# Last expert round of a decoder trunk: scatter by matmul replaced by a DRAM scratch and indirect fetches per token

## What is computed

```python
logits = hf @ router_w + router_b
top_p, top_i = lax.top_k(softmax(logits), 2)          # 2 of 8 experts per token
gates = one_hot(top_i) * (top_p / sum(top_p))
for e in range(8):                                    # D_FF_EXPERT = 3584
    out = out + gates[:, e:e+1] * (silu(hf @ w_gate[e]) * (hf @ w_up[e])) @ w_down[e]
x = x + gate_mod * out                                # gated residual, gate_mod per channel
y = x * rsqrt(mean(x * x, axis=-1) + 1e-6) * final_norm_g
```

## Time and profile before

| | us |
|---|---|
| three runs | 1512.93, 1510.95, 1510.21 |
| median | 1510.95 |
| profiled execution: its span, first to last instruction | 1512.1 |
| TensorE busy, of the span | 1430.2 (95%) |
| last `e_down` (753) starts | 1491.42 |

### The profile page before, as it was taken

How to read it: one execution, slowest core, us unless ns; L and a number is a source line. 1 busy time by engine, 2 the same in 40 slices (tenths; PEclk the granted TensorE clock), 3 DMA queues, 4 the chain that set the end, 5 groups by cost and what they waited for, 6 DMA issues and landing times.

```text
span 1512.1 us, 44722 instructions
## 1 busy us (share of the span) xinstructions
PE 1430.2 (95%) x19890; PEld 1062.4 (70%) x19890; DVE 370.1 (24%) x1021; ACT 159.2 (11%) x378; POOL 137.5 (9%) x230
## 2 busy tenths in 40 slices
PE   4999999999998898999999989989989989999996
PEld 3887888888887787666567757767757755555554
DVE  2816230220203715111111111111111111113334
ACT  2103111101112203100000000000000000000001
POOL 0000043140300000000000000000000000000000
PEclk8999999999999999999999999999999999999999
DMA  9948595646328705759999999999999999999870
GB/s 385 422 165 333 194 372 216 262 188 247 140 84 356 313 0 232 326 193 426 426 421 410 426 426 395 426 426 408 427 425 407 424 427 405 413 426 394 361 308 29
DMA packets 44202, 493.91 MB, mean 327 GB/s; under 512 B 4896, under 2 KB 5152, under 8 KB 5792
## 3 DMA queue, kind: packets, MB, share of 16 engines
q1 hardware_dynamic: 41040, 475.02, 76.4%
q10 hardware_dynamic: 3024, 16.73, 2.7%
HBM read 478.10 MB, written 13.63 MB: 325 GB/s over the span
## 4 chain that ended last, share of the span: by engine, by line
PE 82%; DMA 12%; DVE 4%; ACT 1%; issue 1%; SPq 0%; POOL 0%; DVEq 0%; POOLq 0%
PE PS L744 30%; PE PS L443 20%; PE PS L753 15%; DMA ring<-in_expert_stream 9%; PE PS L598 5%; PE PS L427 2%; DMA arena<-in_expert_stream 2%; DMA ring<-in_dense_stream 2%; PE PS L762 2%; PE PS L724 1%; DVE arena L1052 1%; PE PS L652 1%; PE PS L568 1%; PE PS L580 1%; PE PS L475 1%; PE PS L417 1%
## 5 line engine op out<-in xcount | busy, mean ns | idle before, releaser
L744 PE MATMUL PS<-ring,arena 128*32 128x256 f32 x7040 | 405.4, 381 | 21.7 <-DMA ring<-in_expert_stream 13.1
L744 PEld LDWEIGHTS PS<-ring,arena 128*32 128x32 f32 x7040 | 251.5, 110 | 154.1 <-issue 16.9
L443 PE MATMUL PS<-arena,ring 128*128 128x256 f32 x1408 | 314.2, 384 | 4.3 <-ACT arena L855 2.7
L443 PEld LDWEIGHTS PS<-arena,ring 128*128 128x128 f32 x1408 | 269.9, 193 | 44.5 <-issue 6.3
L753 PE MATMUL PS<-ring,arena 128*32 128x256 f32 x4928 | 298.4, 381 | 0.8 <-DVE consts L1052 0.8
L753 PEld LDWEIGHTS PS<-ring,arena 128*32 128x32 f32 x4928 | 178.6, 111 | 91.4 <-issue 4.4
L744 PE MATMUL PS<-arena 128*32 128x256 f32 x2816 | 162.9, 382 | 10.7 <-DMA arena<-in_expert_stream 7.8
L1052 DVE TENSOR_TENSOR stat<-stat,PS 128x128 f32<-128x128 f32 x154 | 44.4, 288 | 505.3 <-ACT stat L1010 505.3
L1052 DVE TENSOR_TENSOR arena<-arena,PS 128x256 f32 (+1 forms) x123 | 55.3, 449 | 376.3 <-PE PS L443 236.5
L744 PEld LDWEIGHTS PS<-arena 128*32 128x32 f32 x2816 | 101.2, 111 | 63.9 <-DMA arena<-in_expert_stream 9.0
L1602 POOL COPY arena<-arena 128x256 f32 x153 | 61.3, 401 | 817.3 <-PE PS L744 768.8
(11 more groups left out here) (187 smaller groups left out, 603.4 us busy)
## 6 DMA issues: line engine op xcount, KB each, us to landing
ring<-in_expert_stream SPq DMA_DIRECT2D x136, 2048.0 KB, 19.9
ring<-in_dense_stream SPq DMA_DIRECT2D x105, 1024.0 KB, 7.8
arena<-in_expert_stream SPq DMA_DIRECT2D x32, 2048.0 KB, 23.2
ssm_scratch<-arena ACTq DMA_DIRECT2D x12, 1024.0 KB, 5.0
ring<-ssm_scratch SPq DMA_DIRECT2D x12, 1024.0 KB, 9.8
arena<-in_xt ACTq DMA_DIRECT2D x1, 1024.0 KB, 13.9
arena<-in_ssm_small ACTq DMA_DIRECT2D x1, 1024.0 KB, 9.1
out_t<-arena ACTq DMA_DIRECT2D x4, 256.0 KB, 2.6
```

Source lines behind the costliest of these rows:

```text
L443: mm = pe.matmul(PS[:, bank, j * T:(j + 1) * T], w[:, c, j * P:(j + 1) * P], moving[:, c, :], start=(c == 0), stop=(c == NC - 1))
L744: mm = pe.matmul(PS[32 * q:32 * q + 32, 0, 0:256], hbuf[:, c * BLK:(c + 1) * BLK], w[:, q * 256:(q + 1) * 256], start=(c == 0), stop=(c == ...
```

## The change

- **No scatter.** `spread_turn`, `reps`, `gtb`, `gate_rows` and `scatter` go. In the last round `keep` adds to `acc` as in the others, and `scale_block` (VectorE, one 128x256 product per block) multiplies by the per-channel gate `gf_quads`.
- **Gate row.** `gf_quads` is made at the start of round 1: VectorE writes the gate on 8 diagonals (in the first round, in place of `spread`), TensorE multiplies them by ones (8 matmuls, `gate_row`), VectorE copies four quarters out of PSUM.
- **Stores.** After the Silu of block j ScalarE waits for `y_scaled` of block j-1 and issues a DMA of that block (128 rows of 1 KB) to `y_scr`, 896 rows of 4 KB in DRAM, one row per slot. Before, in the dense stage, four DMAs fill `y_scr` with 3.67 MB of `xt_in`, so that every row holds something.
- **Fetch.** When all stores have landed GpSimd issues four indirect DMAs, each of 128 rows of 4 KB (one per token) to `ring`: two tiles of 128 tokens, two picks each. TensorE meanwhile transposes the residual to token rows (16 transposes, `turn_resid`).
- **Mix and norm, token by token.** VectorE: four products with add of 128x1024. ScalarE: Square with its sum along the row, then Sqrt of 128x1. VectorE: reciprocal of 128x1, two products of 128x512 per tile. Four output DMAs.

```diff
 # TensorE
-            def scatter(first=False, last=False):
-                for h in range(2):
-                    for q in range(4):
-                        rows = slice(BLK * q, BLK * q + BLK)
-                        mm = pe.matmul(PS[:, 4 + q, h * T:(h + 1) * T], accb[rows, h * P:(h + 1) * P], gtb[rows, :],
-                                       start=(first and h == 0), stop=last, skip_group_check=True)
+            def turn_resid():
+                for tt in range(2):
+                    for c in range(NC):
+                        mm = pe.transpose(PS[:, 4 + 2 * tt + c // 4, (c % 4) * P:(c % 4 + 1) * P], B[:, c, tt * P:(tt + 1) * P], ident)
+                mm.then_inc(x_turned, 1)
...
                         e_down(at)
-                        if rnd == ROUNDS - 1:
-                            pe.wait_ge(gt_ready, j)
-                            scatter()
...
 # ScalarE
+            for n in range(-(-MOST * BLK // T)):
+                rows = min(T, MOST * BLK - n * T)
+                act.dma_start(y_scr[n * T:n * T + rows, :], xt_in.rearrange("p (h d) -> (p h) d", d=D)[0:rows, :]).then_inc(y_filled, 16)
...
+            def store_block(j):
+                act.wait_ge(y_scaled, j + 1)
+                act.dma_start(y_scr[bass.ds(j * BLK, BLK), :].rearrange("i (q n) -> q i n", q=4),
+                              acc[:, bass.ds(j * 256, 256)]).then_inc(y_stored, 16)
...
+            with act.Fori(1, upto[-1]) as j:
+                act.wait_ge(gu_done, j + upto[-1] * (ROUNDS - 1) + 1)
+                silu().then_inc(silu_ready, 1)
+                store_block(j - 1)
+            store_block(upto[-1] - 1)
...
 # VectorE, last round
                     dve.wait_ge(down_done, j + blocks * rnd)
-                    if rnd < ROUNDS - 1:
-                        keep(wide_block(acc, j - 1), rnd).then_inc(acc_done, 1)
+                    keep(wide_block(acc, j - 1), rnd).then_inc(acc_done, 1)
                     dve.wait_ge(e_hid, j + blocks * rnd + 1)
                     turn_hid().then_inc(hidT_ready, 1)
                     if rnd == ROUNDS - 1:
-                        dve.wait_ge(e_scat, j + 1)
-                        keep_last(j - 1)
-                        dve.wait_ge(gt_ready, j)
-                        gate_rows(j - 1)
+                        scale_block(j - 1)
...
+            dve.wait_ge(x_turned, 1)
+            for t_ in range(2):
+                dve.wait_ge(y_back[t_], 16)
+                link(dve.scalar_tensor_tensor(y_mix[t_], y_rows[2 * t_], r2[6][:, t_:t_ + 1],
+                                              PS[:, 4 + 2 * t_:6 + 2 * t_, :].rearrange("p b n -> p (b n)"), ALU.mult, ALU.add))
+                dve.wait_ge(y_back[2 + t_], 16)
+                dve.scalar_tensor_tensor(y_mix[t_], y_rows[2 * t_ + 1], r2[7][:, t_:t_ + 1], y_mix[t_], ALU.mult,
+                                         ALU.add).then_inc(mixed_ready, 1)
...
 # GpSimd, behind its last block copy
+            pool.wait_ge(down_done, upto[-1] * ROUNDS)
+            pool.wait_ge(y_stored, upto[-1] * 16)
...
+            for t_ in range(2):
+                for k in range(2):
+                    pool.indirect_dma_start(out=y_rows[2 * t_ + k], out_offset=None, in_=y_scr[:, :],
+                                            in_offset=bass.IndirectOffsetOnAxis(ap=slots_i[:, 2 * k + t_:2 * k + t_ + 1], axis=0)
+                                            ).then_inc(y_back[2 * k + t_], 16)
```

More of the change, by code:

```diff
@@ L248, in trunk_kernel @@
         hg = arena[:, 0:MOST * 256]
-        h_tm, sel, places, spread = more[:, 0:2048], more[:, 2048:3840], more[:, 3840:4736], more[:, 4736:5760]
+        h_tm, sel, places = more[:, 0:2048], more[:, 2048:3840], more[:, 3840:4736]
         o = 0
@@ L265, in trunk_kernel @@
         over, nbs = take(48), [take(8) for _ in range(3)]
+        att_sum = take(4)
         slot_of = [take(2) for _ in range(2)]
@@ L727, in gather, with gate_row @@
                 mm.then_inc(e_gather, 1)
[L729 to L735, removed]
+            def gate_row():
+                pe.wait_ge(diag_ready, 1)
+                for c in range(NC):
+                    mm = pe.matmul(PS[:, 2 + c // 4, (c % 4) * P:(c % 4 + 1) * P], ones, g_diag[:, c * P:(c + 1) * P], start=True, stop=True)
+                mm.then_inc(gf_psum, 1)
             def gate_up(at, fresh):
@@ L773, in _ @@
             for rnd in range(ROUNDS):
-                if rnd == ROUNDS - 1:
-                    pe.wait_ge(part_zeroed, 1)
-                    pe.wait_ge(reps_ready, 1)
-                    scatter(first=True)
+                if rnd == 1:
+                    gate_row()
                 for e in range(EXPERTS):
@@ L812, in _ @@
             e_down(expert_at(ROUNDS - 1, EXPERTS - 1))
[L814 to L821, removed]
+            pe.wait_ge(hg_ready, GATHERS)
+            turn_resid()
         @block.scalar
@@ L1027, in _ @@
                     silu().then_inc(silu_ready, 1)
-            for rnd in range(1, ROUNDS):
+            for rnd in range(1, ROUNDS - 1):
                 with act.Fori(0, upto[-1]) as j:
@@ L1454, in _ @@
             link(tt(r2[7], r2[5], r2[6], ALU.mult))
[L1455 to L1458, removed]
+            for k in range(2):
+                s = dve.tensor_copy(slots_i[:, 2 * k:2 * k + 2], slot_of[k])
+            s.then_inc(slots_ready, 1)
+            dve.wait_ge(mod_taken, 5)
+            for c in range(NC):
+                s = dve.tensor_scalar(g_diag[:, c * P:(c + 1) * P], ident, part(3, 2)[:, c:c + 1], None, ALU.mult)
+            s.then_inc(diag_ready, 1)
             def col(a, at):
@@ L1475, in keep, with scale_block @@
                 return tt(dst, dst, PS[:, 1, 0:256], ALU.add)
[L1477 to L1486, removed]
+            def scale_block(j):
+                dve.wait_ge(acc_done, blocks * (ROUNDS - 1) + j + 2)
+                tt(wide_block(acc, j), wide_block(acc, j), gf_quads, ALU.mult).then_inc(y_scaled, 1)
             dve.wait_ge(items_ready, 1)
@@ L1501, in _ @@
                 turn_hid().then_inc(hidT_ready, 1)
[L1502 to L1505, removed]
+                if rnd == 1:
+                    dve.wait_ge(gf_psum, 1)
+                    for q in range(4):
+                        s = dve.tensor_copy(gf_quads[32 * q:32 * q + 32], PS[32 * q:32 * q + 32, 2 + q // 2, q % 2 * 256:(q % 2 + 1) * 256])
+                    link(s)
                 with dve.Fori(1, blocks) as j:
@@ L1515, in _ @@
                     if rnd == ROUNDS - 1:
[L1516 to L1519 removed]
+                        scale_block(j - 1)
             dve.wait_ge(down_done, blocks * ROUNDS)
[L1521 to L1526, removed]
[L1527 to L1535 removed]
+            keep(wide_block(acc, blocks - 1), ROUNDS - 1).then_inc(acc_done, 1)
+            scale_block(blocks - 1)
+            dve.wait_ge(x_turned, 1)
[6 more added lines that the diff above has]
+                                         ALU.add).then_inc(mixed_ready, 1)
+            dve.wait_ge(mixed_ready, 2)
+            dve.wait_ge(gain_loaded, 16)
+            for t_ in range(2):
+                dve.wait_ge(root_ready, t_ + 1)
+                link(dve.reciprocal(row_rms[:, t_:t_ + 1], row_rms[:, t_:t_ + 1]))
+                for h in range(2):
+                    at = slice(h * 512, (h + 1) * 512)
+                    dve.scalar_tensor_tensor(ring[:, FINAL + t_ * D + h * 512:FINAL + t_ * D + (h + 1) * 512], y_mix[t_][:, at],
+                                             row_rms[:, t_:t_ + 1], gain_row[:, at], ALU.mult, ALU.mult).then_inc(final_ready, 1)
         @block.gpsimd
```

87 lines of the change are left out of this document (46 added, 41 removed).

## The result

| | us |
|---|---|
| before, five runs | 1510.61 median (1510.21 to 1512.93) |
| changed, five runs | 1521.79 median (1516.3 to 1527.01) |
| ratio changed to before | 1.0076, 95% interval 1.0053 to 1.0099 |
| profiled execution of the changed kernel | 1521.79, span 1520.0 |

The change makes the kernel 0.8% slower: 11 us in the median, 7.9 us between the two profiled spans. The forecast was 1517.0 with 0.49 for slower. Changed and before differ by little, but the same 8 us can come from very different parts, so the result is read stage by stage.

What follows compares the result with a forecast made beforehand. Weights were taken to bound the rounds up to the last, TensorE the last (6.40 us per block). Last store landed at 1502 plus an end of 16.1 gives span 1518.1; the median, 1.1 lower, is 1517 us, range 1491 to 1533.

Steps and rivals of the forecast that it cites:

- the likeliest case: Last round: stores on four engines lag behind the weights, ScalarE's issue not blocking; last landing 1502, result 1517 us; chance 0.53.
- Taken from TensorE: Last round: without the scatter 18 blocks take 5.18 us, not 6.40, saving 22.0 us, plus 1.1 in the last block.
- Four engines: Block stores: the destination's 4 outermost put 32 packets on each of four engines, 1.92 us of them per block.
- 1 KB at 60 ns: Block stores: assumed price per 1 KB packet, between bounds of 38 and 87 ns, giving 42.2 us of stores.
- New wait on ScalarE: Store issue between Silus: 3.3 us of work before the next Silu at 5.18, free unless the issue blocks on a full queue.
- queue full: Rival, last round: stores pile up, ScalarE's issue blocks Silu and TensorE, weights come late; result 1531 us; chance 0.14.
- even spread: Rival, block stores: all 16 engines carry each store, 0.48 us of each engine; result 1493 us; chance 0.27.
- The end: From the last store's landing to the span's end: four fetches 8.0 us, then VectorE and ScalarE work; 16.1 us in all.
- At nothing: Earlier stages: the 8.6 us scratch fill and the gate row cost no time, hidden by 21 us free and weight waits.
- ScalarE's issue longer than 1 us and gaps before Silu (queue full): Sign on ScalarE in the last round that would show the likeliest case wrong and the queue full.
- GpSimd waiting about 25 us after the last `e_down`: Sign at the kernel's end that would show the likeliest case right: GpSimd waits about 25 us for stores.

Runs made afterwards that it cites:

- with the stores late: Changed kernel with all 22 block stores (4x32x256 form) issued after the last Silu instead of one after each; 1518.38 us.
- the flat store: Changed kernel, still one DMA per block, but its destination is one run of 128 rows (output wrong, for time only); 1493.2 us.
- the halves: All stores after the last Silu, each cut into two DMAs of 64 partitions with 2 outermost in the destination; 1548.75 us, one run.
- the two spread forms: Changed kernel with each block's store as four DMAs of 32 partitions (1492.1 us), or as one DMA with a flat destination (1493.2 us).

## Why the prediction was right, and where it was not

**The sign was right, and so was its root, a store on four engines. The way by which it costs time was wrong in the likeliest case, and that the size came out is luck.** 1517.0 was forecast, 1521.79 measured, inside the range. Step by step:

- *Taken from TensorE: right.* 18 x 1.22 + 1.1 = 23.1 us were forecast. Without stores 22.8, with the stores late 124.2 - 101.45 = 22.75.
- *Four engines: right.* It was read from the shapes in the program, no trace before having such a transfer, and the packet counts, the flat store and the halves bear it out.
- *1 KB at 60 ns: too dear.* It measured 45 to 47. The four engines then owe the stores 22 x 32 x 0.046 = 32.4 us, not 42.2.
- *New wait on ScalarE: the step that failed.* "It costs nothing while the issue does not block on a full queue", and the likeliest case took it that the issue does not. It does, in four of 22 blocks: 22.6 us of TensorE idle, in three of them, and 7.7 at a lower clock. The forecast let the stores lag freely and put the last landing at 1502. It came at 1501.70, but by another way: the last store was issued only at 1497.72 and landed 3.98 us later, since by then the queue was empty. Two errors cancelled, the dear packet and the missing stops. With the measured packet, and without blocking, the sum as the prediction made it gives 1354.07 (pair 147's landing in this run) + 98.4 + 32.4 + 2.0 = 1486.9 for the last landing, 15 us before the one measured, and 1505.2 for the span; no run here has four engines and an issue that does not block, so that figure is only worked out.
- *The rival "queue full": right in mechanism, too high.* It had 0.14. It said that ScalarE stands at the issue with Silu and TensorE behind it, and that weights come late too. The first is what the chain shows; of late weights there is little (1.5 us of TensorE's waits). It put the last store at 1512 to 1520 and the result at 1531, since it let the stores pile up to the end. In the run each stop of TensorE holds back the releases of the weights' slots too, the weights pause (22.1% of the DMA time from 1390 to 1398 against 98%), and in that pause the small packets go at their own price: from 1393 to 1397 388 of them take 27.2% of 16 x 4 us, 45 ns each. The stop clears its own cause, until the next.
- *The rival "even spread": right in price.* 1493 was worked out; 1492.1 and 1493.2 measured for the two spread forms. By stages it holds too for the four DMAs: 118.1 us from pair 147's landing to the last store's, 119 forecast (1478 - 1359), and an end of 18.6 for 16.1. The chance of 0.27 was for the store as written, which is not spread.
- *The end: 2.2 us short.* 16.1 us were forecast from the last landing; it took 1520.0 - 1501.7 = 18.3. The rows are below.
- *At nothing: right for the fill and the gate row.* In 160 to 240, where the fill runs, TensorE is busy for 40.00 of 40.00 us twice. The gate row's matmuls run from 746.7 to 748.5, ahead of the wait for weights in round 1, and the gate-up behind that wait starts at 765.48 where it started at 765.87.

Windows of the changed kernel where the fill runs, to be held against the earlier trace rows:

```profile
160.00:200.00 40.00, 40.00 (x352) 34.96 (x351) 8.55 (x20) 9.73 (x17) 9.85 (x9) 1.00 0.70 267
200.00:240.00 40.00, 40.00 (x358) 34.64 (x357) 11.43 (x14) 4.09 (x9) 8.28 (x4) 1.00 0.95 381
```

The DMA share rises by 0.06 and 0.12: 40 x 0.18 = 7.2 us in these two stretches, near the 8.6 forecast for the fill, and 21 us were free.

The end in the changed kernel, timeline of GpSimd:

```profile
1502.72 1.17 POOL L1638 DMA_INDIRECT ring<-y_scratch,slots_i  x1 [15.34 <-POOLq L1633]
1504.18 0.94 POOL L1638 DMA_INDIRECT ring<-y_scratch,slots_i  x1 [0.30 <-issue]
...
1506.67 0.93 POOL L1638 DMA_INDIRECT ring<-y_scratch,slots_i  x1 [0.31 <-issue]
```

and of VectorE:

```profile
1507.29 1.28 DVE L1536 SCALAR_TENSOR_TENSOR ring<-ring,arena,PS 128x1024 f32<-128x1024 f32 x1 [9.84 <-DMA ring<-y_scratch,slots_i]
...
1512.24 1.28 DVE L1539 SCALAR_TENSOR_TENSOR ring<-ring,arena 128x1024 f32<-128x1024 f32 x1
```

The fetches start 1.46, 1.24 and 1.25 us apart, near the 1.2 forecast. But the last product starts at 1512.24, 10.5 us after the last landing and not 8.0: one us passes between landing and first issue (semaphores on GpSimd), and from there 4.6 us to the first product, where 1.2 + 1.2 + 2.0 was taken. From the first product to the last it is 4.95 us and not 3 x 1.2: the second product waits for its rows (it starts 2.28 us after the first), and the other two follow at VectorE's pace, some 1.33 each. Then 4.7 us to VectorE's end (4.3 forecast) and 3.1 to the span's end (3.6).

**The signs to look for, that the prediction named.** "ScalarE's issue longer than 1 us and gaps before Silu (queue full)" was the row that decided it, and it was there. "GpSimd waiting about 25 us after the last `e_down`" was not: it waits 6.2 us. Blocks at 5.18 us between the stops, no scatter, and a DMA share of 0.24 from 1460 to 1490 were there as said; the stores' landing is not in the profile of this kernel.

**The best version** with a right output is the store in four DMAs of 32 partitions: 1492.1 us, 19 us (1.3%) under the kernel before. It keeps the design of the change and alters how each store is cut.

## What to carry to other kernels

Look at the outermost dimension of both sides of every DMA that the kernel waits for or that shares the engines with a stream: a store with 4 outermost ran on four of 16 engines here, and the same bytes in four DMAs of 32 rows, or flat, made 30 us of difference. A DMA issue on an engine that also computes was free here only while few packets were pending; count what the queue must hold when each of its packets waits for a large one of another queue, and put nothing that TensorE needs behind it. And when two errors can cancel, check a forecast by where its intermediate times come from and not by whether they agree.

## What the runs showed that had not been expected

- **One packet for one, 1 KB against 16 KB.** An engine serves q1 and q10 in equal numbers of packets: 23.6 to 23 in the changed kernel, 22 to 22 with the flat store. Small packets among large ones cost the large stream little (2% of the time), but they go at its pace: by the counts 32 of them take 18.6 us, against 1.5 us alone.
- **How much a queue holds** is not settled. All four issues that stopped in the changed kernel began with 93 to 100 packets per engine pending and 33 more to come (22 issues of 33 packets, less the packets of q10 up to then): at the 5th store 132 had been issued and 38 served. But the 6th store's issue went through in 0.58 us at 98 pending, and the 16th's at 115, when the weights paused or had ended. With nothing beside them (all stores late) the issues from the third on stayed at 0.58 us up to 126 pending and took 0.7 to 1.35 from there, with 129 to 142 pending. No one number fits these. That the stops come from too many pending packets is shown by the spread forms, which never had over 49 pending and no stop; how the queue counts them is open.
- **An issue's own price depends on its shape:** 0.58 us for the destination with 4 outermost, 0.345 for the flat one, 0.33 for a quarter of 32 partitions.
- **The clock adds to a stop.** Pauses of TensorE of 6.0, 10.7 and 5.9 us made the next gate-up 5.33, 6.50 and 6.20 us, in place of 3.45, at a granted clock of 0.68, 0.55 and 0.58; the `e_down` behind each took its usual 1.73 at a clock of 1.00 again. At 1.2 GHz, the lower of the two levels, the 64 would take twice 3.45 = 6.9 us, so most of each ran at it. The length of the pause does not give the price: 6.0 and 5.9 us cost 1.9 and 2.7. A quarter of the loss (7.7 of 30.3 us) is this.
- **The stretches up to 1360 shift by some us from run to run** in kernels that don't differ there: pair 147 landed between 1351.9 (flat store) and 1359.0 (before). The stages above were therefore compared by their own length and not by their start. The cause was not looked for.
